# Two reduced-precision products instead of one fp32 product for the head and group sums of squares in a hybrid decoder block

## What is computed

```python
def rmsnorm(x, g):
    y = x * rsqrt(mean(x * x, axis=-1) + NORM_EPS)
    return y * g

q = rmsnorm(q.reshape(bsz, t, ATT_HEADS, ATT_HEAD_DIM), q_norm)    # 8 heads x 64
k = rmsnorm(k.reshape(bsz, t, ATT_HEADS, ATT_HEAD_DIM), k_norm)
...
y = y.reshape(bsz, t, D_SSD) * silu(z)
y = rmsnorm(y.reshape(bsz, t, SSD_GROUPS, D_SSD // SSD_GROUPS), norm_g)    # 2 groups x 512
```

## Time and profile before

| | |
|---|---|
| median of 3 runs | 2114.91 us (2110.85 to 2115.95) |
| the profiled execution | 2112.15 us |
| its span | 2110.1 us |
| PE busy | 2099.2 us, 99% |
| DVE busy | 1572.2 us, 75% |
| POOL busy | 1276.1 us, 60% |
| ACT busy | 1008.6 us, 48% |
| matmuls of the head sums (L719) | 16 records for 8 products |
| matmuls of the group sums (L829) | 4 records for 2 products |

### The profile page before, as it was taken

The page is one execution under the profiler, slowest core; times in us unless marked ns, Lnnn a source line. Parts: engine busy times, 40 slices in busy tenths (PEclk is TensorE's granted clock), DMA queues, the critical chain, the costliest instruction groups (busy, mean ns, idle before and its releaser), DMA issues.

```text
span 2110.1 us, 34267 instructions
## 1 busy us (share of the span) xinstructions
PE 2099.2 (99%) x11280; PEld 1771.3 (84%) x11280; DVE 1572.2 (75%) x2805; ACT 1008.6 (48%) x1468; POOL 1276.1 (60%) x731
## 2 busy tenths in 40 slices
PE   9999999999999999999999999999999999999999
PEld 7777777887888888888888888888888888888888
DVE  6589565557663226888888888888888899988987
ACT  6343334434433446555545545555555544444543
POOL 5345334444454666676767767767767676666665
PEclk9999999999999999999999999999999999999999
DMA  6224123233333444354454544544544766655743
GB/s 211 84 74 126 61 70 99 96 101 104 103 99 125 145 143 141 124 176 135 157 166 134 169 158 143 173 147 144 169 150 148 251 229 212 211 186 189 237 128 132
DMA packets 150118, 308.74 MB, mean 146 GB/s; under 512 B 13272, under 2 KB 54424, under 8 KB 149880
## 3 DMA queue, kind: packets, MB, share of 16 engines
q1 hardware_dynamic: 103568, 250.39, 35.7%
q10 hardware_dynamic: 46440, 56.94, 8.6%
HBM read 261.64 MB, written 45.51 MB: 146 GB/s over the span
## 4 chain that ended last, share of the span: by engine, by line
PE 91%; DVE 6%; issue 1%; DMA 1%; ACT 1%; POOL 0%; ACTq 0%; SPq 0%; DVEq 0%
PE ps L873 39%; PE ps L872 20%; PE ps L684 10%; PE ps L686 9%; PE ps L685 9%; DVE work L1461 1%; DVE work L1460 1%; DVE work L1364 1%; DVE work L1363 1%; PE ps L780 1%; PE ps L766 1%; PE ps L752 0%; DVE work L1452 0%; DVE work L1439 0%; PE ps L821 0%
## 5 line engine op out<-in xcount | busy, mean ns | idle before, releaser
L873 PE MATMUL ps<-comb,fhi 128*128 128x512 f32 x3507 | 1230.4, 393 | 0.0
L872 PE MATMUL ps<-comb,flo 128*128 128x256 f32 x3507 | 984.5, 281 | 0.4 <-POOL flo L632 0.4
L873 PEld LDWEIGHTS ps<-comb,fhi 128*128 128x128 f32 x3507 | 656.8, 187 | 146.2
L632 POOL TENSOR_TENSOR flo<-raw,fhi 128x1024 fp32r<-128x1024 f32 (+2 forms) x252 | 485.0, 1935 | 358.1 <-ACT fhi L1211 357.9
L872 PEld LDWEIGHTS ps<-comb,flo 128*128 128x128 f32 x3507 | 662.0, 189 | 7.8 <-DVE ps L1820 2.9
L602 POOL TENSOR_TENSOR wlo<-raw,whi 128x512 fp32r<-128x512 f32 x260 | 361.1, 1403 | 395.4 <-ACT whi L991 344.8
L632 POOL TENSOR_TENSOR flo<-sum,fhi 128x1024 fp32r<-128x1024 f32 (+2 forms) x168 | 324.0, 1936 | 40.1 <-ACT fhi L1211 39.9
L1211 ACT ACTIVATE fhi<-ps 128x1024 fp32r<-128x1024 f32 (+2 forms) x168 | 141.8, 844 | 421.8 <-DVE ps L1702 225.4
L684 PE MATMUL ps<-hhi,whi 128*128 128x512 f32 x784 | 317.2, 405 | 2.0 <-DVE hlo L1611 2.0
L686 PE MATMUL ps<-hlo,whi 128*128 128x512 f32 x784 | 306.4, 391 | 0.0
L685 PE MATMUL ps<-hhi,wlo 128*128 128x512 f32 x784 | 305.8, 390 | 0.0
(11 more groups left out here) (246 smaller groups left out, 2644.2 us busy)
## 6 DMA issues: line engine op xcount, KB each, us to landing
raw<-w_gu SPq DMA_DIRECT2D x176, 512.0 KB, 3.8
raw<-w_in SPq DMA_DIRECT2D x196, 256.0 KB, 3.3
raw<-w_dn SPq DMA_DIRECT2D x96, 256.0 KB, 3.0
raw<-w_dn SPq DMA_DIRECT2D x64, 320.0 KB, 3.0
act_hi<-pair_sums ACTq DMA_DIRECT2D x20, 896.0 KB, 4.2
act_lo<-pair_sums ACTq DMA_DIRECT2D x20, 896.0 KB, 8.3
raw<-w_out SPq DMA_DIRECT2D x64, 256.0 KB, 3.2
comb<-act_hi SPq DMA_DIRECT2D x21, 512.0 KB, 3.9
```

What stands on the lines that cost most here:

```text
L632: nc.gpsimd.tensor_tensor(flo[s][:, 0:w], src[:, 0:w], fhi[s][:, 0:w].bitcast(F32), ALU.subtract).then_inc(f_lo_pool, 1)
L872: nc.tensor.matmul(dst[:, 0:HT], flo[s][:, w], both[:, HI, :], start=fresh and k == 0, stop=False, skip_group_check=True)
L873: ins = nc.tensor.matmul(dst, fhi[s][:, w], both, start=False, stop=k == n - 1, skip_group_check=True)
```

## The change

The ten fp32 products become pairs of fp32r products that add up in the same bank, with the squares split into a high and a low part.

- ACT squares each q or k tile twice, into `nsq` (fp32) and again into `nhi` (fp32r).
- POOL subtracts, `nlo = nsq - nhi` (`low_square`), right after weight quarter `4 * (m + 7)`, the same one that stands ahead of the squares on ACT. To place it, POOL's loop over the weight quarters is cut in two loops with a piece written out between them. POOL also copies `ones` and `halves` once to fp32r (`sums`).
- `nq_sq` now counts two for each tile, one by ACT and one by POOL. ACT's first square of a tile also waits for POOL's subtraction of the tile before.
- PE multiplies `halves` by `nhi` and by `nlo`.
- For the gated norm DVE copies `gsum` into `ghi` (fp32r) and subtracts it into `glo`, after the fourth tile of a group, and `y_done` counts that tile only after both. PE multiplies `ones` by both.

```diff
+NQ0 = (TILE_OF["q", 0] + 2) // 2
+NQ1 = (TILE_OF["k", 3] + 2) // 2 + 1
...
+            def low_square(m):
+
+                pool.wait_ge(nq_sq, 2 * m + 1)
+                nc.gpsimd.tensor_tensor(nlo[:, m % 2, :], nsq[:, m % 2, :], nhi[:, m % 2, :].bitcast(F32), ALU.subtract).then_inc(nq_sq, 1)
+
+            with pool.Fori(0, NQ0) as i:
+                for q in range(8):
+                    low(q, 8 * i + q, T)
+            pool.wait_ge(const_loaded, 16 * 3)
+            nc.gpsimd.tensor_copy(sums[:, :, :], cm[:, 3:5, :])
+            for n in range(8 * NQ0, 8 * NQ1):
+                low(n % 8, n, T)
+                m = n // 4 - 2 - TILE_OF["q", 0]
+                if n % 4 == 0 and 0 <= m < 8:
+                    low_square(m)
...
-                    pe.wait_ge(nq_sq, m + 1)
+                    pe.wait_ge(nq_sq, 2 * m + 2)
                     if m >= 2:
                         pe.wait_ge(nq_done, m - 1)
-                    nc.tensor.matmul(bank(4 + m % 2), C("halves"), nsq[:, m % 2, :], start=True, stop=True).then_inc(nq_sum, 1)
+                    nc.tensor.matmul(bank(4 + m % 2), exact("halves"), nhi[:, m % 2, :], start=True, stop=False)
+                    nc.tensor.matmul(bank(4 + m % 2), exact("halves"), nlo[:, m % 2, :], start=False, stop=True).then_inc(nq_sum, 1)
...
-                        nc.tensor.matmul(bank(7), C("ones"), gsum, start=True, stop=True).then_inc(gn_sum, 1)
+                        nc.tensor.matmul(bank(7), exact("ones"), ghi[:, :], start=True, stop=False)
+                        nc.tensor.matmul(bank(7), exact("ones"), glo[:, :], start=False, stop=True).then_inc(gn_sum, 1)
...
-                    A(nsq[:, m % 2, :], qkT[:, m, :], ACT.Square).then_inc(nq_sq, 1)
+                    if m:
+                        sc.wait_ge(nq_sq, 2 * m)
+                    A(nsq[:, m % 2, :], qkT[:, m, :], ACT.Square)
+                    A(nhi[:, m % 2, :], qkT[:, m, :], ACT.Square).then_inc(nq_sq, 1)
...
-                            V.tensor_tensor(gsum, gsum, gtmp, ALU.add).then_inc(y_done, 1)
+                            if j2 % 4 < 3:
+                                V.tensor_tensor(gsum, gsum, gtmp, ALU.add).then_inc(y_done, 1)
+                            else:
+                                ch_.link(V.tensor_tensor(gsum, gsum, gtmp, ALU.add))
+                                ch_.link(V.tensor_copy(ghi[:, :], gsum))
+                                V.tensor_tensor(glo[:, :], gsum, ghi[:, :].bitcast(F32), ALU.subtract).then_inc(y_done, 1)
```

More of the change, by code:

```diff
@@ L239, in hybrid_block @@
         x2d = at(yq(6, 1), "x2d", [P, 2, T])
+        nhi = at(EXTRA, "nhi", [P, 2, T], F32R)
+        nlo = at(EXTRA + 4 * KB, "nlo", [P, 2, T], F32R)
+        ghi = at(EXTRA + 8 * KB, "ghi", [P, T], F32R)
+        glo = at(EXTRA + 10 * KB, "glo", [P, T], F32R)
+        sums = at(EXTRA + 12 * KB, "sums", [P, 2, P], F32R)
         ctx.enter_context(nc.sbuf_tensor("reserved", [P, (EXTRA + 16 * KB) // 4], F32))
@@ L245, in C, with exact @@
             return cm[:, CM_NAMES.index(name), :]
+        def exact(name):
+            return sums[:, ("ones", "halves").index(name), :]
         def par(name, j=0, n=1):
@@ L603, in low @@
                                         whi[:, slot % NW, 0:width].bitcast(F32), ALU.subtract).then_inc(lo_ready, 1)
-            with pool.Fori(0, (QN_OUT - 4) // 8) as i:
+            def low_square(m):
[11 more added lines that the diff above has]
+                    low_square(m)
+            with pool.Fori(NQ1, (QN_OUT - 4) // 8) as i:
                 for q in range(8):
```

## The result

The changed kernel takes 2117.36 us (median of 12 runs, 2115.55 to 2121.87), the kernel before 2111.53 us (median of 12 runs, 2109.59 to 2115.95). The ratio is 1.0026, with a 95% interval of 1.0018 to 1.0034: slower, by 5.8 us between the medians. That is just within the 0.3% that the prediction took for the least that can be told from no change; the interval tells it from no change all the same.

A forecast was written before the change was run, and what follows sets the result against it. PE (99% busy) and DVE were both taken as near the critical path; 3.0 slip + 1.5 longer path - 0.6 wait - 0.8 group products = + 3.1 us on 2114.9, giving 2118.0 us, range 2109.5 to 2124.0.

The forecast's parts named there:

- slower rival: DVE's slip compounds or PE's clock falls behind a wait: + 6 to + 9 us, 2121 to 2124; chance 0.12.
- What PE saves: At ten products on PE: 0.40 us each (0.86 to 0.46), 3.2 for head and 0.8 for group products, 4.0 in all.
- What the path gains: Read-out to head product: second square and subtraction add 1.89 us; at m = 7 about 1.5 shows after the 0.40 saved.
- What DVE loses to POOL: DVE's two-input instructions wait for POOL's: slip at m = 7 of 1.8 + 2.0 - 0.8 = 3.0 us.
- The wait at the second v tile goes: PE's 0.61 us wait for DVE at the second v tile's transposes vanishes, cutting 4.5 us to 3.9.
- The group sums fit by 0.2 us: Group norm: DVE's copy and subtraction take some 1.2 us against 1.44 to PE's product, so no wait.
- What would show it: PE waits for POOL at m = 3 to 7, longest 2 to 3 us, together 5 to 9; L1439's mean towards 1660 ns.
- PE's saving: Rival: DVE slips by - 0.8 to 0.5, total - 0.7 to + 0.6 us; in part 0.28, in full or beyond 0.07.
- that rival: PE's fp32r pair is no cheaper than the fp32 product it replaces: about + 5 us, 2120; chance 0.03.
- The exclusive lock: SBUF port pair of DVE and POOL locks for whole instructions; shared bandwidth would give slip 1.3 instead of 3.0 us.
- the prediction's sign of being wrong: On PE: a low clock showing behind a wait, one of four listed signs that would make the prediction wrong.

The follow-up runs named there:

- run 3: Changed kernel with the head norms' high part alone: one ACT square, one fp32r product, no subtraction; ratio to the kernel before 0.9995, MLP's first product at 810.1 us.
- run 4: Kernel before with only the two group sums made as pairs, head norms unchanged; ratio to the kernel before 1.0005, MLP's first product at 810.7 us.
- run 8: Changed kernel with head pairs for m = 3 to 7 alone, m = 0 to 2 as before; read-out of m = 7 at 179.56 us, MLP at 813.5.
- run 7: Changed kernel with head pairs for m = 0 to 2 alone, the others as before; read-out of m = 7 at 180.97 us, MLP at 814.2.
- run 1: Changed kernel without POOL's head-norm subtraction, PE multiplying the high part twice; ratio to the kernel before 1.0008, MLP's first product at 813.4 us.
- run 12: Kernel before with group pairs and, for m = 3 to 7, PE's pair behind further ACT squares, no POOL subtraction; m = 7 at 175.76 us, MLP at 809.7.
- run 5: Changed kernel, same instructions placed later: ACT's second square, POOL's subtraction, PE's pair, ACT's Ln and Exp; ratio to the kernel before 0.9999, MLP at 812.2 us.
- run 2: Changed kernel with POOL's subtraction kept but PE not waiting for it, multiplying the high part twice; ratio to the kernel before 1.0021, MLP at 815.9 us.

## Why the prediction was right, and where it was off

It was right in direction, in the range, and in the mechanism: PE and DVE are both near the bound in the stage of the head norms, and the change puts POOL work against DVE's. The forecast of + 3.1 us was too small, by the medians (+ 5.8) and by the trace (+ 5.1). Both lie just above the + 1.5 to + 5 to which it gave its chance of 0.50, and below the + 6 of its slower rival, in a gap between the ranges that it gave. That 2118.0 stands close to 2117.36 is in part luck: the median of before was 2114.91 from three runs and 2111.53 from twelve.

- *What PE saves*, 0.40 us each: right, 0.46 against 0.86. Runs 3 and 4 add that 0.6 of the 0.8 us count at the group sums, and little at the head sums.
- *What the path gains*, 1.89 us: right. The subtraction at m = 4 ends at 147.06 + 1.27 = 148.33, that is 3.22 us after the read-out's start at 145.11, against 3.24.

```profile
147.06 1.27 POOL L618 TENSOR_TENSOR nlo<-work,nhi 128x512 fp32r<-128x512 f32 x1 [3.27 <-ACT nhi L1038]
```

- *What DVE loses to POOL*: this is the step that was mis-sized. It gave 3.0 us at m = 7 and 5.08 was measured. Its count for m = 3 to 7, 1.8, is what run 8 shows (1.93). Its count for m = 0 to 2, "2.0 us for it, less 0.8 that DVE gets from PE's first two savings", 1.2 us, is 3.34 in run 7. It looked at one place, 115.30, where it saw the 2.0 rightly. It missed the place before, at 98.24, where 1.6 us are lost, and took it that DVE follows PE up to there and gains. By the read-out of m = 2 DVE was 1.42 us late (114.84 against 113.42) and not 0.8 early, which is the whole miss. The loss did not fade, since PE, ACT and DVE pass the indexer's heads to each other in a circle: ACT's relu waits for DVE's sums, and PE in the end for ACT, at a product that started at 115.82 and without a wait before:

```profile
101.27 0.49 ACT L1107 ACTIVATE work<-ps 128x384 f32<-128x384 f32 x1 [1.07 <-DVE work L1482]
117.25 1.61 PE L766 MATMUL ps<-work 64*128 64x512 f32 x4 [1.33 <-ACT work L1107]
```

  Without the subtraction (run 1) that read-out is 0.36 us late.
- *The wait at the second v tile goes*: right. Attention starts 5.7 us later: 6.95 at the last pair, less the 0.4 saved there, less 0.6 for that wait, less 0.2 to 0.3 us elsewhere.
- *The group sums fit by 0.2 us*: right, 0.25. One wait on the way to the next y product grew from 0.9 to 1.2 us, which takes 0.3 of their 0.8 and which the prediction did not have.
- *What would show it*: waits at the pairs of 5 to 9 us in sum, the longest 2 to 3: 6.3 and 2.7. That they began at m = 3: right. L1439 averaged 1323 ns before; its eight records after are two at 0.75 and six at 1.66 to 1.67, a mean of 1.43 us: the way that was forecast, and less than "towards 1660", since one scaling that met POOL before (120.94) no longer does (125.17). ACT's extra waits for POOL's subtraction are seven and not ten, which changes nothing.
- *The rivals.* PE's saving did not come through, for the reason given against it. The pair is cheaper than the product (0.46 us), so that rival is out. The slip did compound once, through the indexer as above, but not in every tile. No clock fell in the changed kernel's profile, though PE stood for 2.70 us at once: the stretch around it, with the granted clock as the third number from the right,

```profile
143.00:155.00 12.00, 9.30 (x41) 7.33 (x41) 11.59 (x19) 5.31 (x9) 7.17 (x5) 1.00 0.24 74
```

shows 1.00. So the gaps of which the Trainium skill warns ("TensorE: Matmul & The Clock Gate", "HAM oscillation — how this bites in real kernels") cost this execution nothing. In most others of the changed kernel the clock was a little lower, which is in the last section.

The exclusive lock (the Trainium skill, "SBUF — State Buffer", "SBUF: two separate sides") was the right model. Between 100 and 190 us of the trace after, L1394 and L1469 take a whole turn, 1.66 or 1.67 us, or none, 0.69 or 0.75, and nothing between. Only L1393, the first of the three, which can arrive within a running POOL instruction, takes from 0.94 to 1.74.

Left open: a kernel that keeps the exact pair and puts POOL's weight quarters behind DVE's three instructions, as run 12 did by accident, wasn't tried. Runs 5 and 12 suggest it, and neither shows it.

## What to carry to other kernels

Before trading one engine's time for another's, look at who feeds whom in that stretch: here PE was 99% busy over the kernel, and a saving of 5.8 us on it was worth 1.4, since DVE was as full in just those tiles. POOL's idle time is not free where DVE runs instructions with two SBUF inputs, or the one-input TENSOR_SCALAR of run 5. What a POOL instruction costs depends on which of them it meets, so place it among instructions that the trace shows at the same length beside POOL and without it, as the read-outs from PSUM (0.69 us) here, and look at every such meeting in the trace, the first one above all. Where a new wait carries a large number in the profile, take it away before believing it: the 6.3 us here were worth 0.7.

## What the runs showed that was not expected

- Longer ACT work ahead of POOL's block made DVE faster (run 12: 1.87 us by m = 7).
- A one-input fp32 instruction of DVE (TENSOR_SCALAR, 128x384) took 1.17 us beside POOL's subtraction and 0.36 without it (run 5).
- The clock does fall, in some executions. Over the whole span its mean was 0.998 or 0.999 in ten of the twelve executions of the changed kernel, in eight of ten of run 2 and in six of eleven of run 3, and 1.000 in seventy of the seventy-three of the kernel before that ran beside the experiments. It shows no cost: the three of the changed kernel with 0.998 took 2115.55, 2116.09 and 2119.45 us, the two with 1.000 took 2118.04 and 2121.87. Where it fell is known for one execution alone. In the profile of run 2 PE waited 1.3 us for ACT, like the changed kernel at the same place, and then the granted clock went down for some 3 us:

```profile
117.00:120.00 3.00, 2.72 (x8) 1.53 (x9) 2.64 (x2) 1.83 (x4) 2.56 (x2) 0.87 0.00 0
120.00:123.00 3.00, 3.00 (x9) 2.37 (x8) 2.90 (x6) 1.63 (x3) 1.38 (x2) 0.56 0.31 87
123.00:126.00 3.00, 3.00 (x14) 2.44 (x13) 2.93 (x4) 0.00 (x0) 1.58 (x1) 1.00 0.34 97
```

  In between matmuls stand 0.43 us apart (the 1.2 GHz level) instead of 0.23. It cost nothing by the read-out of m = 3 (130.76 in both kernels). In the changed kernel's profile the same wait left the clock alone. So the prediction's sign of being wrong, a low clock behind a wait, is absent from the changed kernel's profile, and whether it shows behind these waits in its other executions is open.
